# Two blocks on one core: the second mixer's steps in another order, queries' norms in the exponential's scale, and level scores in 64x64 halves

## What is computed

```python
# first mixer, per head, chunks of tokens: q_, k_, decay from a running product of forget gates
attn = einsum('bhtk,bhtsk,bhsk->bhts', q_, decay, k_)
o = o_inter + einsum('bhts,bhsv->bhtv', attn, v_)
# second mixer, 6 heads, 128 + 64 dimensions, causal
q = (rms_norm(cq, qa_g) @ w_uq).reshape(B, S, 6, 192)
kv = (rms_norm(ckv, kva_g) @ w_ukv).reshape(B, S, 6, 256)
k = concat([kv[..., :128], broadcast(kpe)]); v = kv[..., 128:]
q = rms_norm(q, qn_g); k = rms_norm(k, kn_g)          # then rotary on the last 64
s = where(causal, q k^T * 192 ** -0.5, -inf); o = softmax(s) @ v
# memory attention beside it: 4 heads of 64, 256 keys, softmax(q k^T / 8) @ v
x = x + concat([y, m]) @ w_out
```

## Time and profile before

| what | us |
|---|---|
| median of 3 runs | 1977.81 (1977.66 to 1979.5) |
| profiled execution, its own time | 1975.79 |
| its span, first to last instruction | 1974.0 |
| TensorE busy | 1880.5 (95%) |
| VectorE, ScalarE, GpSimd busy | 910.5, 732.2, 726.3 |
| granted TensorE clock over the span | 0.971 of full |
| levels stage, 178.51 to 265.13 | 86.62 |
| second mixer from its first scores, 809.20 to 950.11 | 140.91 |

### The profile page before, as it was taken

How to read it: one execution, slowest core, us unless ns; L and a number is a source line. 1 busy time by engine, 2 the same in 40 slices (tenths; PEclk the granted TensorE clock), 3 DMA queues, 4 the chain that set the end, 5 groups by cost and what they waited for, 6 DMA issues and landing times.

```text
span 1974.0 us, 23904 instructions
## 1 busy us (share of the span) xinstructions
PE 1880.5 (95%) x9265; PEld 1513.9 (77%) x9265; DVE 910.5 (46%) x1301; ACT 732.2 (37%) x965; POOL 726.3 (37%) x226
## 2 busy tenths in 40 slices
PE   7999988999999999898999999998899999999998
PEld 5789963788888887565788888886787778878876
DVE  5235654355564116565255555114516744413453
ACT  4132134355555224443355555222214542221323
POOL 2253730344443344212144434343223424443321
PEclk9999996999999999898999999999999999999999
DMA  7632110132322322111022232223122122323121
GB/s 270 239 107 86 43 43 0 65 107 85 106 85 80 103 94 92 46 43 43 28 101 100 91 106 72 97 93 121 64 77 41 59 71 85 113 92 107 64 86 43
DMA packets 28661, 170.27 MB, mean 86 GB/s; under 512 B 2992, under 2 KB 5296, under 8 KB 12208
## 3 DMA queue, kind: packets, MB, share of 16 engines
q1 hardware_dynamic: 25200, 151.20, 22.5%
q10 hardware_dynamic: 3392, 18.09, 2.8%
HBM read 167.18 MB, written 2.10 MB: 86 GB/s over the span
## 4 chain that ended last, share of the span: by engine, by line
PE 70%; issue 16%; DVE 7%; POOL 4%; ACT 2%; DMA 0%; POOLq 0%; DVEq 0%; ACTq 0%
PE ps L383 42%; PE ps L700 11%; POOL wlo L1015 4%; PE ps L599 2%; PE ps L401 1%; PE ps L402 1%; PE ps L403 1%; DVE scr L2021 1%; PE ps L936 1%; PE ps L946 1%; PE ps L919 1%; PE ps L947 1%; PE ps L948 1%; DVE prm L2009 1%; PE ps L673 1%
## 5 line engine op out<-in xcount | busy, mean ns | idle before, releaser
L1015 POOL TENSOR_TENSOR wlo<-wraw,whi 128x2048 fp32r<-128x2048 f32 (+3 forms) x153 | 648.3, 4237 | 1106.1 <-ACT whi L1131 1088.2
L383 PE MATMUL ps<-hh,whi 128*128 128x512 f32 x1344 | 527.2, 392 | 2.3 <-DVE sig L2191 1.6
L383 PE MATMUL ps<-hl,whi 128*128 128x512 f32 x1344 | 523.1, 389 | 0.0
L383 PE MATMUL ps<-hh,wlo 128*128 128x512 f32 x1344 | 523.0, 389 | 0.0
L1131 ACT ACTIVATE whi<-wraw 128x2048 fp32r<-128x2048 f32 (+3 forms) x149 | 264.9, 1778 | 427.0 <-PE ps L383 339.7
L383 PEld LDWEIGHTS ps<-hh,whi 128*128 128x128 f32 x1344 | 252.3, 188 | 58.4 <-issue 3.6
L383 PEld LDWEIGHTS ps<-hh,wlo 128*128 128x128 f32 x1344 | 252.3, 188 | 52.8
L383 PEld LDWEIGHTS ps<-hl,whi 128*128 128x128 f32 x1344 | 252.4, 188 | 52.6 <-issue 1.2
L1861 DVE SCALAR_TENSOR_TENSOR scr<-ps,vec,scr 128x510 f32<-128x510 f32 (+1 forms) x176 | 120.2, 745 | 93.1 <-ACT scr L1324 93.1
L700 PE MATMUL ps<-gh,whi 128*128 128x512 f32 x352 | 137.1, 389 | 1.3 <-DVE gl L1876 1.3
L700 PE MATMUL ps<-gh,wlo 128*128 128x512 f32 x352 | 137.0, 389 | 0.0
(11 more groups left out here) (422 smaller groups left out, 2868.4 us busy)
## 6 DMA issues: line engine op xcount, KB each, us to landing
wraw<-in_w SPq DMA_DIRECT2D x63, 1024.0 KB, 4.9
wraw<-in_w0b SPq DMA_DIRECT2D x26, 1024.0 KB, 4.9
wraw<-in_w1o SPq DMA_DIRECT2D x26, 1024.0 KB, 4.9
wraw<-in_wd SPq DMA_DIRECT2D x32, 704.0 KB, 4.0
ada<-in_wada ACTq DMA_DIRECT2D x12, 1024.0 KB, 7.0
xtok<-in_x SPq DMA_DIRECT2D x4, 512.0 KB, 8.0
out<-ytok SPq DMA_DIRECT2D x2, 1024.0 KB, 4.2
wraw<-in_w SPq DMA_DIRECT2D x3, 576.0 KB, 3.9
```

The lines of the kernel that those rows point to most:

```text
L383: last = mm(o, l, r, start=(k == 0 and n == 0), stop=(k == K - 1 and n == 2))
L1015: nc.gpsimd.tensor_tensor(wlo[:, s % 2, 0:wd], wraw[:, s % 2, 0:wd], whi[:, s % 2, 0:wd].bitcast(F32), ALU.subtract).then_inc(lo_ready, 1)
```

## The change

- Levels: level 0 stays. In levels 1 to 6 each 128x128 product becomes two of 64 weight columns and 64 moving columns, for the two diagonal 64x64 blocks; level 7 makes only the block of first keys by second queries.
- Order: TensorE's iteration n is jobs, transposes n-1, scores n+1, values n-1. ScalarE's is exponentials n, jobs, copies n-1. VectorE's is maximum n, first job, scaling n, other jobs, taking of an odd head. The first scores stand before the loop.
- The probabilities have two buffers, the second where two constants were, which move. These are cast before the first scores.
- Jobs: 12 a pair, listed by hand in `JOBS`, so that jobs of the next pair stand between those of one. The queries are no longer multiplied by their norms. Job 9 instead transposes the norms (four transposes); VectorE copies 8 columns to `rqt`; the step's maximum is multiplied by them, and the exponential takes them as its scale. The keys are multiplied by the product of both gains.
- Values (jobs 5 and 6) are taken from PSUM by ScalarE instead of VectorE, counted by a new semaphore. `emptied` is raised once a pair by VectorE (job 2), and by three by ScalarE after its last iteration.

```diff
-    prm, ptm = at("prm", HR + 12 * KB, [P, 2, T]), at("ptm", HR + 16 * KB, [P, 2, 4, P])
+    prm = [at("prm0", HR + 12 * KB, [P, 2, T]), w("prm1", 12, [P, 2, T])]
+    ptm = at("ptm", HR + 16 * KB, [P, 2, 4, P])
...
-        HOST = (2, 2, 2, 2, 2, 2, 2, 2, 3, 2, 2, 3, 4, 2, 4, 0, 0, 0, 0, 0)
+        JOBS = (((0, 0), (0, 1), (0, 2)),
+                ((0, 3), (0, 4)), ((0, 5), (0, 6)), ((0, 7), (0, 8)), ((1, 0), (0, 9)),
+                ((1, 1), (0, 10)), ((1, 2), (0, 11)), ((1, 3), (1, 4)), ((1, 5), (1, 6)),
+                ((1, 7), (1, 8), (2, 0)), ((1, 9), (1, 10), (2, 1)), ((1, 11), (2, 2), (2, 3)), ((2, 4), (2, 5), (2, 6)),
+                ((2, 7), (2, 8)), ((2, 9), (2, 10)), ((2, 11),), (), (), (), (), ())
...
-                            last = mm(ps[:, h, t], hk[:, h, t], hq[:, h, t], start=True, stop=True)
...
+                            elif k < 7:
+                                mm(ps[0:64, h, t], hk[:, h, t], hq[:, h, t], start=True, stop=True)
+                                last = mm(ps[64:128, h, u], hk[:, h, u], hq[:, h, u], start=True, stop=True)
+                            else:
+                                last = mm(ps[0:64, h, u], hk[:, h, t], hq[:, h, u], start=True, stop=True)
...
+                elif k == 9:
+                    pe.wait_ge(m_rs, pr + 1)
+                    for x in range(4):
+                        last = nc.tensor.transpose(ps[:, bank, x * P:(x + 1) * P], rstd4[:, x * P:(x + 1) * P], cc("ident"))
...
             for n in range(21):
                 if n < 20:
-                    if n:
-                        pe.wait_ge(g_ex, 2 * n)
...
-                    step_scores(n).then_inc(g_sc, 1)
...
+                    for pr, k in JOBS[n + 1]:
+                        job(pr, k)
...
-                if n < 20:
-                    for j in hosted(n):
-                        job(j)
+                if n < 19:
+                    pe.wait_ge(g_ex, 2 * n + 2)
...
+                    step_scores(n + 1).then_inc(g_sc, 1)
                 if n:
                     pe.wait_ge(g_pt, 2 * n)
                     step_pv(n - 1).then_inc(g_pv, 1)
...
+                    for a in range(2):
+                        tt = 2 * (k - 5) + a
+                        last = A(mv[:, tt, pr * 256:(pr + 1) * 256], ps[:, FB + place(pr, k) % 2, 256 * a:256 * a + 256], ACT.Copy,
+                                 scale=rtok[:, tt:tt + 1])
+                    last.then_inc(v_ev, 1)
...
+                        A(prm[n % 2][:, e, 0:wd], ps[:, e, 0:wd], ACT.Exp, bias=nmx[:, c:c + 1], scale=rqt[:, q:q + 1] if n >= 8 else 1.0,
+                          accum_out=sm[:, c:c + 1]).then_inc(g_ex, 1)
...
                     for e in range(2):
                         hi(oh1[:, 2 * (n // 4 - 3) + e, :])
+            act.wait_ge(v_ev, 6)
+            act.sem_inc(emptied, 3)
...
+                elif k == 9:
+                    q = 8 * pr
+                    V.tensor_copy(rqt[:, q:q + 8].rearrange("p (i e) -> p i e", e=2),
+                                  b.rearrange("p (i g t) -> p i g t", i=4, t=32)[:, :, 0:2, 0]).then_inc(m_ev, 1)
...
+                    STT(out=mkn[:, h, :], in0=mkn[:, h, :], scalar=qkn, in1=b, op0=ALU.mult, op1=ALU.mult)
+                    TT(mkr[rows, pr, :], kr0[rows, :], b[rows, :], ALU.mult).then_inc(m_ev, 1)
...
+                    link(V.tensor_reduce(nmx[:, c:c + 2], ps[:, 0:2, 0:wd], AX, ALU.max, negate=True))
+                    TT(nmx[:, c:c + 2], nmx[:, c:c + 2], rqt[:, q:q + 2], ALU.mult).then_inc(g_mx, 1)
...
+                for i, (pr, k) in enumerate(JOBS[n + 1]):
+                    if i == 1:
+                        norm(n)
+                    job(pr, k)
+                if len(JOBS[n + 1]) < 2:
+                    norm(n)
```

More of the change, by code:

```diff
@@ L290, in sqbuf, with place, taken, finished @@
             return sqacc if i % 2 == 0 else sqx[:]
-        NJ, FB = 13, 2
-        HOST = (2, 2, 2, 2, 2, 2, 2, 2, 3, 2, 2, 3, 4, 2, 4, 0, 0, 0, 0, 0)
[L295 to L307, removed]
+        FB = 2
+        JOBS = (((0, 0), (0, 1), (0, 2)),
[4 rows of a table added]
+        FLAT = sum(JOBS, ())
+        def place(pr, k):
+            return FLAT.index((pr, k))
+        def taken(pr, k):
+            return sum(j not in (5, 6, 8) for _, j in FLAT[:place(pr, k) + 1])
+        def finished(pr, k):
+            return sum(j not in (2, 6) for _, j in FLAT[:place(pr, k) + 1])
         def chunks(n):
@@ L724, in _, with job @@
             last.then_inc(used, 1)
-            def job(j):
-                pr, k = j // NJ, j % NJ
-                bank = FB + j % 2
+            def job(pr, k):
+                i = place(pr, k)
+                bank = FB + i % 2
                 s = S_UQ + 2 * pr
-                if j < 2:
+                if i < 2:
                     pe.wait_ge(emptied, S_Z1 + 3)
-                elif k == 10:
-                    pe.wait_ge(m_rs, pr + 1)
-                else:
-                    pe.wait_ge(m_ev, taken(j - 2))
+                else:
+                    bp, bk = FLAT[i - 2]
+                    if bk == 8:
+                        pe.wait_ge(m_rs, bp + 1)
+                    elif bk in (5, 6):
+                        pe.wait_ge(v_ev, 2 * bp + bk - 4)
+                    else:
+                        pe.wait_ge(m_ev, taken(bp, bk))
                 if k < 3:
@@ L835, in _ @@
                         for c in range(chunks(n - 1)):
[L836 removed]
+                            last = nc.tensor.transpose(ps[:, 4 + e, c * P:(c + 1) * P], prm[(n - 1) % 2][:, e, c * P:(c + 1) * P], cc("ident"))
                         last.then_inc(g_tp, 1)
[L838 to L840 removed]
+                if n < 19:
+                    pe.wait_ge(g_ex, 2 * n + 2)
+                    if n >= 7 and n % 4 == 3:
+                        pe.wait_ge(m_ev, taken(n // 4 - 1, 11))
+                        pe.wait_ge(m_rp, 2 * (n // 4) + 2)
+                    step_scores(n + 1).then_inc(g_sc, 1)
                 if n:
```

153 lines of the change are left out of this document (76 added, 77 removed).

## The result

The kernel after takes 1967.86 us (median of 5 runs, 1963.94 to 1970.16), the kernel before 1977.66 (5 runs, 1976.83 to 1979.50): ratio 0.995, 95% interval [0.9939, 0.9961]. It is faster by 9.8 us, where no change was forecast; the range ended at 1968.5. The profiled execution took 1967.27 us with a span of 1965.3, 8.7 less than before.

What follows compares the result with a forecast made beforehand. It took TensorE as the bound: levels limited by matmul work, the mixer by waits and the low clock. Levels -9, mixer +5.8 and tail +3.0 sum to -0.2 us: 1977.6 us, no change, range 1968.5 to 1986.5.

Steps and rivals of the forecast that it cites:

- work 107.2: Second mixer: TensorE's busy time at 2.4 GHz, 122.5 less 13.5 for low clock and 1.8 for changed jobs, in us.
- clock 11.5: Second mixer: low clock costs what it does now, 13.5 us, less 2 hidden under waits.
- tail 3.0: First output slot waits for the count ScalarE now raises after rounding heads 4 and 5: +3.0 us.
- Levels: Levels stage: both halves run at once, TensorE work falls 18 us, waits for GpSimd take part back: -9 us.
- Rival 1: Levels: the halves follow one another and only level 7 gains, 2.6 us; +6, 1984 us; chance 0.08.
- (c): Mixer's last seven steps, with little or no job left to cover each step's chain: 13.7 us of added waits.
- (a): Mixer's memory steps: values wait for ScalarE's copies behind exponentials, evictions and roundings; 9.5 us over eight steps.
- (b): Mixer: four single waits where VectorE's scaling blocks a job behind it or exponentials are late; 5 us.
- rival 3: Mixer steps with jobs: TensorE stays at 2.4 GHz, clock costs 4 rather than 11.5 us; 1970 us; chance 0.17.
- rival 4: Mixer: ScalarE is less late, (a) and (b) are 7 rather than 14.5 us; 1970 us; chance 0.12.
- Rival 2: Mixer from step 13 on: the low clock holds, 5 to 8 us more than charged; 1984 us; chance 0.22.
- the signs named as proof against the forecast: Prediction wrong if the tail is absent, mixer waits stay under 20 us, or the granted clock there is 1.00.

Runs made afterwards that it cites:

- levels_alone: The kernel before with only the diff's level products, 64x64 halves instead of 128x128; 1967.21 us.
- values_vector: The kernel after with the evictions of the values moved back from ScalarE to VectorE; 1964.86 us.
- no_scaling: The kernel before without VectorE's scaling of the probabilities, so that transposes wait for the exponentials alone; 1956.47 us.

## Why the prediction was wrong

**The sum.** Mixer and tail were predicted at 149.7 us: work 107.2, waits 28, clock 11.5, tail 3.0. The trace has 138.1: work 111.4, waits 21.1, clock 3.4 (half of 6.8 busy), tail 2.2. The levels came out 1.5 us above the prediction in this trace, and the stretch between the stages is 1.7 longer, with 3.4 us more at the low clock and 0.9 more of waits at the same work. -0.2 + 4.2 - 6.9 - 8.1 - 0.8 + 1.5 + 1.6 = -8.7, the difference of the spans.

**Levels: right.** Predicted -9, measured -7.5 with 3.4 us of low clock in level 0 (its group lasts 7.22 us instead of 5.5), -9.2 at equal clock and -10.2 in the median of levels_alone. A pair costs 0.12 us (24 pairs with 96 records in 2.96), group 2.9 instead of 2.7; the waits stand before levels 3, 5 and 7. Dropped work is 14.7 us instead of 18, given back 5.4 instead of 8, so two errors nearly cancel. Two slips of the working change nothing: keys ready at 9.0 against 8.2 make a wait of 0.8, not 1.1 (it was 0.86), and levels 4 and 5 gain 2.7 by its own count, not 3.0. Rival 1 falls.

**Waits of the mixer: places right, sum 7 too high.** (c) was nearly right, one by one: 1.56, 0.43, 1.44, 0, 3.20, 1.63, 2.20 and 0.74 (11.2) against 2.3, 0.3, 1.4, 1.5, 3.2, 1.7, 2.4 and 0.9. (For steps 13 and 17 the working gives 3.8 less 1.2 or 0.3, so 2.6 and 3.5, and not the 2.3 and 3.2 that it adds.) (a) is 6.1 instead of 9.5, in six steps of eight and 1.85 at most, where I took 1.0 us a step without a row. (b) is 3.8 instead of 5, and 2.21 of it is the held product, which no part of the prediction has: it priced it at 0.2. That VectorE's products wait for GpSimd stood in rows 5, and was used for the levels alone. It was in the waits that go, too. In the kernel before:

```profile
825.69 2.40 POOL L1015 TENSOR_TENSOR wlo<-wraw,whi 128x1024 fp32r<-128x1024 f32 x1
825.80 2.44 DVE L2009 TENSOR_SCALAR prm<-prm,small 128x256 f32<-128x256 f32 x1
```

This scaling takes 0.35 us where GpSimd is idle. The transposes behind it start at 828.29, after 1.06 us of waiting; those at 815.60 and 855.98 (1.53 and 2.18 us of waiting) stand behind one of 1.52 and one of 2.70 us, held in the same way. The new order doesn't end this (2.44 us again at 819.29), but a scaling a step ahead holds nobody up.

**The step that failed: "the low clock follows waits now, and afterwards there are more of them; I charge what it costs now".** Waits rose and low clock fell from 30.7 to 6.8 us (6.8 to 13.7 in the traces with the same mixer, so 3.4 to 6.8 us of cost against the 11.5 charged; 17.1 in values_vector). In the old order long waits stand in steps whose work is light: no_scaling, in which the scaling and its waits go, drops 17 us of low clock. That the mix of light work and waits is what counts is argued from this, not shown. The new order has light and dense jobs mixed up to step 12, and its two low parts (896.4, 920.2) come with the waits of 1.56 and 3.20 us behind that. That is what rival 3 had, with 0.17 (clock cost 4 instead of 11.5), and rival 4 was half true at the same time ((a) and (b) 9.9 us instead of 14.5). Each alone lay inside the range; that both could hold at once was not reckoned with. Rival 2 fell: two waits of 3.20 and 1.63 us in a row, at 920 and 927, left 3.4 us at the low clock, not 30. A term of 11.5 us with bounds of 0 and 20 was the largest uncertainty, and I set it to its present value although each of its rows was tied to a wait that goes.

**Work: wrong sign.** "Two are left, and four transposes come: -0.6 a pair" took 1.13 us for two jobs as 0.57 for one. The two that are left cost 1.12 each, since they stand alone: 2.25 + 0.6 instead of 2.26 us, +0.6 for each pair of heads. That makes +1.8 of the 2.4 us; the rest isn't traced to a cause.

**Tail: right** in place and releaser, 2.2 instead of 3.0.

Of the signs named as proof against the forecast none appeared: the tail is there and the waits are 21.1 us without it. They did not test the clock, the term on which the sum hung, except at a value of 1.00.

## What to carry to other kernels

Before charging a clock penalty for future waits, tie each present low part to its wait and ask whether that wait survives; give the term its own sign to check. A duration of neighbours that run side by side isn't two halves: ask who the neighbour will be afterwards. Where VectorE's operations differ in length for the same shape, look at what GpSimd does meanwhile. In an in-order queue, what feeds TensorE next goes ahead of what is only bookkeeping: three such moves brought 19.9 us in the medians, twice what the whole change did; 15.2 of them are the stage's in the trace, the rest came in stretches that they don't touch.

## What the runs showed of the hardware that was not expected

- Two products that use all rows but different halves of the columns run side by side when they are neighbours, and one after another when they are sorted (records 0.03 against 0.06 us apart on average).
- One-row products reading different rows do the same when neither waits: two in 1.13 us, one alone in 1.12.
- A VectorE operation on two tensors in the buffer waits for a running tensor operation of GpSimd even if it is tiny: 128x2 took 2.01, 3.21 and 4.22 us instead of 0.16. A 128x1 tensor with a per-partition scalar didn't wait (0.33 us for two), a 128x256 one did (2.44 and 2.70 us instead of 0.35).
- The granted clock fell behind 12 us with 0.07 us of waits, and stayed at 1.00 over 16.3 us with 0.11 (both no_scaling).
